# First loads in smaller parts, the first pair's weights split earlier, and one new wait on GpSimd

## The reference

```python
proj = x @ w_in                       # 1024 -> 9216 columns: queries, keys, values, gates ...
kv = mem @ w_mem_kv                   # 256 x 1024 times 1024 x 1024: memory keys, memory values
branches = (y_sb, y_pool, y_lru, y_xa)   # stick-breaking attention, pooling, a recurrence, attention on mem
gates = jax.nn.sigmoid(merge.reshape(b, s, N_BRANCH, d))
merged = gates[:, :, 0] * (branches[0] @ w_branch[0])
for n in range(1, N_BRANCH):
    merged = merged + gates[:, :, n] * (branches[n] @ w_branch[n])
out = merged @ w_out
return layer_norm(DN_ALPHA * x + out, ln_g, ln_b)
```

## Time and profile before

| | |
|---|---|
| median of 3 runs | 2335.09 us (2335.03 to 2335.95) |
| the profiled execution's own time | 2335.42 us |
| its span, first to last instruction | 2333.6 us |
| TensorE busy | 2309.1 us (99%) |
| VectorE, ScalarE, GpSimd busy | 1421.7, 1060.8, 1229.7 us |
| mean DMA rate | 117 GB/s |

### The profile page before, as it was taken

The page is one execution under the profiler, slowest core; times in us unless marked ns, Lnnn a source line. Parts: engine busy times, 40 slices in busy tenths (PEclk is TensorE's granted clock), DMA queues, the critical chain, the costliest instruction groups (busy, mean ns, idle before and its releaser), DMA issues. The chain is left out here.

```text
span 2333.6 us, 30065 instructions
## 1 busy us (share of the span) xinstructions
PE 2309.1 (99%) x10928; PEld 1905.9 (82%) x10928; DVE 1421.7 (61%) x1654; ACT 1060.8 (45%) x1659; POOL 1229.7 (53%) x847
## 2 busy tenths in 40 slices
PE   8999999999999999999999999999999999999998
PEld 5888888888878888888788888888888778888887
DVE  6566642764496466458877777723844695366475
ACT  4555532342475255331566676632342673355220
POOL 1666643864366345445466565644763566445331
PEclk9999999999999999999999999999999999999999
DMA  5544422124213312364344544322133114312442
GB/s 201 198 155 162 144 84 95 54 82 131 91 59 122 131 50 68 109 261 154 110 153 136 165 152 136 109 90 77 55 127 129 50 57 141 117 55 79 146 168 81
DMA packets 99186, 273.19 MB, mean 117 GB/s; under 512 B 9312, under 2 KB 30944, under 8 KB 98016
## 3 DMA queue, kind: packets, MB, share of 16 engines
q1 hardware_dynamic: 97600, 266.56, 34.5%
q10 hardware_dynamic: 1440, 4.72, 0.6%
HBM read 208.33 MB, written 62.91 MB: 116 GB/s over the span
## 5 line engine op out<-in xcount | busy, mean ns | idle before, releaser
L2170 POOL TENSOR_TENSOR WLS<-SR,WHS 128x512 fp32r<-128x512 f32 x264 | 415.0, 1590 | 158.6 <-ACT WHS L1051 152.4
L725 PE MATMUL J<-XBH,WHS 128*128 128x512 f32 x1152 | 453.4, 394 | 1.0 <-DVE XBL L1583 0.6
L727 PE MATMUL J<-XBH,WLS 128*128 128x512 f32 x1152 | 449.2, 390 | 0.0
L726 PE MATMUL J<-XBL,WHS 128*128 128x512 f32 x1152 | 449.0, 390 | 0.0
L725 PE MATMUL J<-XBH,WH 128*128 128x512 f32 x864 | 342.5, 396 | 2.5 <-DVE XBL L1583 1.7
L727 PE MATMUL J<-XBH,WL 128*128 128x512 f32 x864 | 337.0, 390 | 0.0
L726 PE MATMUL J<-XBL,WH 128*128 128x512 f32 x864 | 336.7, 390 | 0.0
L725 PEld LDWEIGHTS J<-XBH,WHS 128*128 128x128 f32 x1152 | 216.4, 188 | 47.2 <-ACT LU L1133 1.6
L727 PEld LDWEIGHTS J<-XBH,WLS 128*128 128x128 f32 x1152 | 216.2, 188 | 46.0
L726 PEld LDWEIGHTS J<-XBL,WHS 128*128 128x128 f32 x1152 | 216.5, 188 | 43.1
L1616 DVE TENSOR_TENSOR ST<-J,ST 128x512 f32<-128x512 f32 x160 | 109.4, 685 | 231.4 <-PE J L727 184.3
(11 more groups left out here) (331 smaller groups left out, 4826.2 us busy)
## 6 DMA issues: line engine op xcount, KB each, us to landing
RAW<-w SPq DMA_DIRECT2D x144, 512.0 KB, 3.7
pk_m<-MB SPq DMA_DIRECT2D x56, 512.0 KB, 5.1
MB<-pk_m SPq DMA_DIRECT2D x48, 512.0 KB, 4.0
KC<-pk_k SPq DMA_DIRECT2D x40, 512.0 KB, 5.4
VC<-pk_v SPq DMA_DIRECT2D x40, 512.0 KB, 4.5
BRAW<-w SPq DMA_DIRECT2D x64, 256.0 KB, 5.2
XRAW<-xt SPq DMA_DIRECT2D x8, 1024.0 KB, 12.8
pk_v<-STL SPq DMA_DIRECT2D x16, 512.0 KB, 5.1
```

Of the source, the lines that this page charges most:

```text
L725: nc.tensor.matmul(to, wh, xh, start=first, stop=True, skip_group_check=True)
L726: nc.tensor.matmul(to, wh, xl, start=False, stop=True, skip_group_check=True)
L727: return nc.tensor.matmul(to, wl, xh, start=False, stop=True, skip_group_check=True)
L2170: low = G_.tensor_tensor(WLS[:, k, :], SR[:, k, :], WHS[:, k, :].bitcast(F32), ALU.subtract)
```

## The change

Four things are changed, all of them in the first 80 us.

1. MRAW is loaded in four parts, not two, and MW of the first head in two parts, not one. TensorE waits for each part where it uses it.
2. The loads of RAW for pair one stand in front of the MW of the third and fourth heads.
3. ScalarE splits RAW of pair one (`first_tile`) before the second head's keys (`keys_of(1)`). VectorE makes the three sums first, then WL, and only then the low part of the second head's keys.
4. GpSimd's first sum for pair two waits until all 14 low parts of x are made.

```diff
-            sp.dma_start(MRAW[:, 0:KD // 2], memt[:, 0:KD // 2]).then_inc(m_in[0], 16)
-            load_mw(0)
-            sp.dma_start(MRAW[:, KD // 2:], memt[:, KD // 2:]).then_inc(m_in[1], 16)
+            def load_memory(i):
+                s = slice(i * KD // 4, (i + 1) * KD // 4)
+                sp.dma_start(MRAW[:, s], memt[:, s]).then_inc(m_in[i], 16)
+
+            def load_first(part, made):
+                s = slice(part * KD // 2, (part + 1) * KD // 2)
+                sp.dma_start(MW[:, 0, s].rearrange("p k n -> p (k n)"), w8[0, :, part * D // 2:(part + 1) * D // 2]
+                             ).then_inc(made, 16)
+
+            load_memory(0)
+            load_first(0, mw_first)
+            load_memory(1)
+            load_first(1, big_raw[0])
+            load_memory(2)
+            load_memory(3)
             load_mw(1)
+            load_w(0, 0)
+            load_w(0, 1)
             load_mw(2)
             load_mw(3)
-            load_w(0, 0)
-            load_w(0, 1)
             for j in range(2):
                 load_x(0, j)
...
             for h in range(HEADS):
-                pe.wait_ge(big_raw[h], 16)
+                pe.wait_ge(big_raw[h] if h else mw_first, 16)
                 for k in range(KD):
-                    if h == 0 and k % (KD // 2) == 0:
-                        pe.wait_ge(m_in[2 * k // KD], 16)
+                    if h == 0 and k % 2 == 0:
+                        pe.wait_ge(m_in[k // 2], 16)
+                    if h == 0 and k == KD // 2:
+                        pe.wait_ge(big_raw[0], 16)
...
             keys_of(0)
+            first_tile(0)
             keys_of(1)
-            first_tile(0)
             sums_of(0, False)
...
             keys_rest(0)
+            first_sums(False)
+            rest_of_first(0)
             keys_rest(1)
-            rest_of_first(0)
-            first_sums(False)
             rest_of_sums(0, False)
...
+                if g == 1 and j == 0:
+                    pool.wait_ge(x_lo, NU)
                 pool.wait_ge(w_raw[0] if j else w_raw[1], 16 * (g + 1))
```

More of the change, by code:

```diff
@@ L305, in build @@
         c_in, c_made, exp_l, small = sem("c_in"), sem("c_made"), sem("exp_l"), sem("small")
-        m_in = [sem(f"m_in{i}") for i in range(2)]
+        m_in, mw_first = [sem(f"m_in{i}") for i in range(4)], sem("mw_first")
         mk_hi, mk_kept = sem("mk_hi"), sem("mk_kept")
```

## The result

The changed kernel takes 2338.48 us (median of 22 runs, 2337.05 to 2340.21), the kernel before 2335.39 us in the same sessions (22 runs, 2334.65 to 2337.12): ratio 1.0013 with an interval of 1.0007 to 1.0019. That is 3.1 us slower. The forecast was 2336.1 with a range up to 2338.3, so the time lies just beyond the range, on the slow side. The profiled execution took 2339.55 us for a span of 2337.8 us, 4.2 longer than before. It lies 1.1 us over the median of its 22 runs, so the trace shows somewhat more loss than the medians do.

A forecast was written before the change was run, and what follows sets the result against it. TensorE, busy 2309.1 of 2333.6 us, bounds the kernel. Early gains (−1.3, −3.5 in all) given back at VectorE's queue, −1.6 at 60 us, +2.6 at 76: +1.0, forecast 2336.1, range 2333.1 to 2338.3.

The forecast's parts named there:

- The start: TensorE's first matmuls: with smaller first loads they begin at about 4.7 us instead of 5.97.
- no wait comes back in the first head: First head's keys: later load quarters land before TensorE needs them, so all four heads end 1.3 us earlier.
- The first loads: Loads at the start: half-long rows delay all loads behind by 0.2 us, between nothing and a tenth of 3.9.
- VectorE's queue as the place where the early gain is lost: Near 31 us: the queue starts when the small load lands, so most of the 3.5 us gain is lost.
- The gain itself: Memory values on TensorE: reached at 26.6 us instead of 30.09, a gain of 3.5 us.
- GpSimd's chain: Pair two's weight sums: six operations start at 52.6 us and end at 62.1, between 61.5 and 63.
- the rule of the Trainium skill that the prediction names: VectorE instructions with two SBUF inputs and GpSimd instructions reading SBUF exclude each other for a whole instruction.
- WLS and STL: TensorE waits 2.5 us for weight sums at pair two's third unit, and 2.6 us at the second transposes.
- the sum said +1.0: Whole program: early gains given back, −1.6 at 60 us and +2.6 at 76 us make +1.0 us.
- partly covered by the wait at 76: Transposes: the wait at 76 us partly covers a clock loss at 58; two full falls unlikely, 0.03.
- The rival with 0.10: TensorE's clock falls in the new waits, costing 2.1 us: 2338.2, or 2340.3 with both; chance 0.10.
- Whether 2.5 us are enough no row here shows: New TensorE waits: a long enough wait would lower the clock to 1.2 GHz; whether 2.5 us suffice stayed open.

The follow-up runs named there:

- two: The kernel before with only the smaller first loads (memory in four, first head's weights in two): 2336.99 us, ratio 1.0004.
- nine: The changed kernel with whole first loads, the four stores ahead of pair three's loads, and CRAW and PRM ahead of x's second half: 2332.43 us, ratio 0.9983.
- one: The changed kernel with the first loads whole again, all else as changed: 2336.86 us, ratio 1.0006.
- six: The changed kernel with whole first loads and the four stores of memory keys and values ahead of pair three's loads: 2334.68 us, ratio 0.9995.
- seven: The same as six but without GpSimd's wait for the low parts of x: 2335.54 us, ratio 0.9998.
- ten: The same as nine but without GpSimd's wait for the low parts of x: 2333.87 us, ratio 0.9990.
- three: The changed kernel without GpSimd's wait for the low parts of x: 2336.88 us, ratio 1.0003.
- four: The kernel before with GpSimd's wait for the low parts of x as its only change: 2338.32 us, ratio 1.0008.
- five: The changed kernel with the four stores of memory keys and values ahead of both loads of pair three: 2335.86 us, ratio 1.0002.
- after: The changed kernel itself, with all four changes, against the kernel before: 2338.48 us, ratio 1.0013.
- before: The kernel without the change: median 2335.39 us beside the changed kernel, 2335.90 to 2336.06 beside the twelve follow-up kernels.
- eight: The kernel before with the memory in eight loads of 128 KB and the first head's weights whole: 2336.67 us, ratio 1.0005.
- eleven: The kernel before with six first loads of 256 KB cut by partitions, 64 rows of 4 KB each: 2337.89 us, ratio 1.0006.
- twelve: The kernel before with the small loads ahead of x's second half and the stores ahead on SP: 2335.77 us, ratio 1.0000.

## Why the prediction was wrong

**The start.** TensorE at 4.37 for 4.7: right. That no wait comes back in the first head was wrong by 0.47 us, which costs nothing at the end.

**The first loads: the step that failed.** "Between nothing and a tenth of the 3.9 us that 1.5 MB take, I take the middle, 0.2 us." VectorE's queue came 1.8 us later, and the smaller loads alone cost 1.1 us in the median (two). The bound took the loads to run at 403 GB/s whatever their size, with a tenth as the most that half-long rows could cost, and no row stood behind that tenth. The trace before had no load of 256 KB in this stretch, so it could not be sized from it; the range ought to have been much wider there. With this term alone put right the sum is 2337.7, still inside the stated range: it took the clock as well to leave it.

**VectorE's queue as the place where the early gain is lost.** Right: nothing of it is left at 33 us, and the ninth kernel shows it from the other side. The gain itself was put too high: the memory values start at 28.12, 2.0 us earlier than before, not at 26.6. The smaller loads explain part of this at most, since with whole loads and the same split (one, six, seven, nine, ten) they start between 27.08 and 28.33. The rest was not traced; it costs nothing here, because the queue waits for the small load.

**GpSimd's chain.** Foretold: 9.5 us from the end of the XBL to the end of the last SR. Measured: 54.2 to 63.6, 9.4 us. The SR at 55.72 took 2.07 us and ended 1.16 us behind VectorE's WL, which was under way until 56.63; the one behind it took 1.29. By the rule of the Trainium skill that the prediction names ("SBUF — State Buffer", "Who interferes with whom") it waits for the whole of WL, and this trace agrees.

**WLS and STL.** The two waits are 2.23 and 2.24 us, foretold 2.5 and 2.6. Three, which lacks GpSimd's wait, has neither; four, where it is the only change, has the second in full and the first with 0.57 us; five shows that SP's four stores carry the second. With the loads whole (one) the kernel is 0.95 us over before, where the sum said +1.0. That the clock falls there too does not spoil the agreement: it falls behind the first wait, and the second takes it up, as the prediction said of such a case ("partly covered by the wait at 76").

**The clock.** The rival with 0.10 came true. A fall costs 1.30 us in after and 1.6 in six, not 2.1: that figure came from the very first matmuls, and here the clock came back after 3.4 us. In the profiled execution of after it fell behind the wait for STL and not behind the one for WLS, in those of one and six behind the one for WLS. "Whether 2.5 us are enough no row here shows" was right as far as it went, but 0.10 was too little for two waits that were both longer than any before behind the start.

**In sum.** Two terms failed, the cost of the smaller loads (0.2, measured 1.8) and the clock (left out of the sum, measured 1.3). The forecast had the transposes 1.0 us later than before; in the trace they are 2.43 later, and the clock adds 1.3. With 1.8 in place of 0.2 the sum would have been 2337.7 without the clock and 2339.0 with it; the median is 2338.5.

## What to carry to other kernels

Loads that stand at the head of a long DMA queue are not made cheaper by cutting them: the first engine starts earlier, but every load behind them lands later, and what counts is the engine that waits for the last small one. Before moving work of one engine behind another's, follow what the moved work frees (here the buffer of the next pair's load) and what else stands in the queue that issues it. A wait on TensorE as long as these, 2.1 to 2.2 us, must be priced with a fall of its clock as a likely case, not as a remote one; and since it falls in some executions of a kernel and not in others, one trace without a fall does not show that the kernel is free of it.

## What the runs showed of the hardware

Six loads of 256 KB at the start of the queue, in place of three of 512 KB, brought 266 and 340 GB/s instead of 388 and 406 in the windows 3 to 6 and 6 to 9 us. With rows of 4 KB on half of the partitions it was 246 and 239. Nine loads, eight of them of 128 KB, cost no more than six.

The clock fell to the lower level behind waits of 2.24 us (after and four, at the transposes), 2.08 us (one) and 2.15 us (six, both at the wait for WLS). It did not behind waits of 2.23 us (after and five, at the wait for WLS). So the length of the wait alone does not tell them apart. It fell between 0.1 us before the work's new start and 1.5 us behind it, stayed down for 3.4 us each time, and cost 1.3 us (after) and 1.6 us (six).

Whether it falls differs between executions of one kernel. A mean clock of 0.998 stands on 11 of the 22 runs of after, and of 11 runs each on 7 of one, 8 of four, 5 of five and 6 of six. It stands on none of the 99 runs of before beside the twelve and on none of two, three, seven, nine, ten, eleven and twelve, and on one of eight, its slowest (2340.93 us). In the traces of these five TensorE has a wait of over 2 us: for WLS in one, five and six, for STL in four, for both in after. No trace of the other kernels has one behind the start. The third digit is too coarse to sort the single runs of after and one: in four it divides the times without overlap, in after it does not.
